# Latent attention of a three-layer transformer kernel: a new order of the score sets, the rotated parts and the PSUM copies on TensorE, VectorE and ScalarE

## What is computed

```python
def _mla(h, positions, w_in, q_a_norm_g, w_q_b, kv_a_norm_g, w_kv_b, w_out):
    ...
    q = (_rmsnorm(q_a, q_a_norm_g) @ w_q_b).reshape(b, s, MLA_HEADS, MLA_NOPE + MLA_ROPE)
    q_nope = q[..., :MLA_NOPE]
    q_pe = _rope(q[..., MLA_NOPE:], positions)
    k_pe = _rope(k_pe[:, :, None, :], positions)[:, :, 0]
    kv = (_rmsnorm(c_kv, kv_a_norm_g) @ w_kv_b).reshape(b, s, MLA_HEADS, MLA_NOPE + MLA_V)
    k_nope, v = kv[..., :MLA_NOPE], kv[..., MLA_NOPE:]
    scale = (MLA_NOPE + MLA_ROPE) ** -0.5
    def block(args):
        qn, qp = args
        sc = (jnp.einsum('bqhd,bkhd->bhqk', qn, k_nope, preferred_element_type=f32)
              + jnp.einsum('bqhr,bkr->bhqk', qp, k_pe, preferred_element_type=f32)) * scale
        p = jax.nn.softmax(sc, axis=-1)
        return jnp.einsum('bhqk,bkhd->bqhd', p.astype(v.dtype), v)
    o = _from_blocks(lax.map(block, (_to_blocks(q_nope), _to_blocks(q_pe))))
    o = o.reshape(b, s, MLA_WIDTH) * jax.nn.silu(z)
    return o @ w_out
```

## Time and profile before

| | |
|---|---|
| Median of 3 runs | 2895.57 us (2894.34 to 2899.68) |
| The profiled execution, own time | 2888.15 us |
| Its span in the trace | 2886.3 us |
| TensorE (PE) busy | 2741.3 us, 95% of the span |
| TensorE weight loads (PEld) busy | 2179.3 us, 76% |
| VectorE (DVE) busy | 1691.3 us, 59% |
| ScalarE (ACT) busy | 1320.9 us, 46% |
| Mean granted TensorE clock | 0.982 of full speed |

### The profile page before, as it was taken

One profiled execution on the slowest core, in us unless ns is written; L12 is line 12 of the kernel. 1 busy time (PEld: TensorE's weight loads), 2 busy tenths in 40 slices (PEclk: granted clock), 3 DMA queues, 4 the chain that ended last, 5 costly groups with the idle time before them and its releaser, 6 DMA issues.

```text
span 2886.3 us, 35234 instructions
## 1 busy us (share of the span) xinstructions
PE 2741.3 (95%) x13229; PEld 2179.3 (76%) x13229; DVE 1691.3 (59%) x2268; ACT 1320.9 (46%) x1902; POOL 0.2 (0%) x4
## 2 busy tenths in 40 slices
PE   7999999998899999999999889999999999999998
PEld 4777777776677777877877667666778888888887
DVE  7688888888777544444455635555765434334345
ACT  5676676665323244444443435565534223123233
POOL 0000000000000000000000000000000000000000
PEclk8999999999999999999999999999999999999999
DMA  7311111111445400000021310000311111111112
GB/s 250 110 46 46 35 51 44 51 36 58 152 155 168 141 10 12 14 6 9 7 102 53 111 44 29 24 16 15 103 38 50 45 53 46 50 47 42 53 41 87
DMA packets 218309, 176.78 MB, mean 61 GB/s; under 512 B 9610, under 2 KB 203106, under 8 KB 218210
## 3 DMA queue, kind: packets, MB, share of 16 engines
q1 hardware_dynamic: 216688, 171.07, 18.9%
q10 hardware_dynamic: 1522, 4.37, 0.4%
HBM read 158.12 MB, written 17.30 MB: 61 GB/s over the span
## 4 chain that ended last, share of the span: by engine, by line
PE 78%; DVE 8%; ACT 6%; DVEq 3%; DMA 2%; issue 2%; SPq 0%; ACTq 0%
PE PS L510 18%; PE PS L512 18%; PE PS L511 18%; PE PS L2195 4%; PE PS L1349 4%; PE PS L1336 2%; PE PS L1322 2%; DVE rest L502 1%; PE PS L1326 1%; PE PS L2185 1%; PE PS L2689 1%; PE PS L2702 1%; PE PS L2156 1%; DMA gated<-in_w_ada 1%; PE PS L2713 1%
## 5 line engine op out<-in xcount | busy, mean ns | idle before, releaser
L510 PE MATMUL PS<-h_high,w_high 128*128 128x512 f32 x2096 | 838.2, 400 | 25.3 <-DVE w_low L532 12.8
L512 PE MATMUL PS<-h_high,w_low 128*128 128x512 f32 x2096 | 822.4, 392 | 0.0
L511 PE MATMUL PS<-h_low,w_high 128*128 128x512 f32 x2096 | 822.1, 392 | 0.0
L510 PEld LDWEIGHTS PS<-h_high,w_high 128*128 128x128 f32 x2096 | 397.2, 189 | 115.1 <-issue 16.1
L512 PEld LDWEIGHTS PS<-h_high,w_low 128*128 128x128 f32 x2096 | 396.7, 189 | 85.0
L511 PEld LDWEIGHTS PS<-h_low,w_high 128*128 128x128 f32 x2096 | 397.6, 190 | 80.4 <-issue 1.4
L527 ACT ACTIVATE w_high<-raw_weights 128x1024 fp32r<-128x1024 f32 (+2 forms) x156 | 156.3, 1003 | 371.7 <-PE PS L512 369.3
L532 DVE TENSOR_TENSOR w_low<-raw_weights,w_high 128x1024 fp32r<-128x1024 f32 (+2 forms) x156 | 179.7, 1153 | 98.7 <-ACT w_high L527 98.4
L3336 DVE SCALAR_TENSOR_TENSOR gated<-rest,gated 128x1024 f32<-128x1024 f32 x44 | 56.6, 1286 | 238.1 <-ACT gated L3294 238.1
L1471 ACT ACTIVATE residual<-PS,rest 128x1024 f32<-128x1024 f32 x112 | 123.7, 1111 | 134.7 <-DVE rest L1633 134.6
L871 DVE SCALAR_TENSOR_TENSOR residual<-PS,rest,residual 128x512 f32 (+1 forms) x96 | 70.9, 749 | 171.1 <-PE PS L512 167.5
(11 more groups left out here) (376 smaller groups left out, 4141.3 us busy)
## 6 DMA issues: line engine op xcount, KB each, us to landing
raw_weights<-in_w_in SPq DMA_DIRECT2D x59, 512.0 KB, 4.1
raw_weights<-in_w_up SPq DMA_DIRECT2D x44, 512.0 KB, 3.8
gated<-in_w_ada SPq DMA_DIRECT2D x13, 1536.0 KB, 7.5
raw_weights<-in_w_out SPq DMA_DIRECT2D x24, 512.0 KB, 4.0
residual<-x_kept SPq DMA_DIRECT2D x3, 4096.0 KB, 14.2
rest<-in_ada_w SPq DMA_DIRECT2D x16, 576.0 KB, 4.9
activations<-in_ada_w SPq DMA_DIRECT2D x8, 1024.0 KB, 14.0
x_kept<-residual SPq DMA_DIRECT2D x2, 4096.0 KB, 14.5
```

Of the source, the lines that this page charges most:

```text
L510: e.matmul(out_, wh[:, k, :], xh[:, k, cols], start=first, stop=False)
L511: e.matmul(out_, wh[:, k, :], xl[:, k, cols], start=False, stop=False)
L512: return e.matmul(out_, wl[:, k, :], xh[:, k, cols], start=False, stop=last_k)
```

## The change

Four things are put in another order in the three functions; no instruction is added or taken out, except register moves of the sequencers that go with the order.

1. TensorE: in blocks 4 and 6 the sets Q1 and K1 stand ahead of PV(1) and PV(2) and no longer behind them. In block 2, PV(0) stays ahead of R1.
2. ScalarE: in block 7 of every head but the last, and in block 1 of even heads, the copy of the transposes stands ahead of the next exponential. In block 1 of odd heads the copy stands ahead of the ScalarE part of R0 (behind the exponential, as before).
3. VectorE, odd heads: the VectorE part of R0 goes from block 1 to block 2, behind the maximum there. That of R1 goes from block 2 to block 3, behind the division and ahead of the maximum. `dve_rope` goes from block 3 to 5, and `act_rope` from 3 to 4.
4. VectorE, even heads: `dve_rope` goes from block 1 to 2.

```diff
@@ pe_head
-                if q in (2, 4, 6):
-                    pe_pv(e, t, q // 2 - 1)
+                if q == 2:
+                    pe_pv(e, t, 0)
                 if wanted(t, BEFORE.get(q), more):
                     pe_set(e, t, BEFORE[q])
+                if q in (4, 6):
+                    pe_pv(e, t, q // 2 - 1)
@@ act_head
             for q in range(8):
+                copied = more and (q == 7 or (q == 1 and not t.odd))
+                if copied:
+                    act_evac(e, t, q)
                 if q < 7:
                     act_exp(e, t, q + 1)
...
-                if wanted(t, BEFORE.get(q), more):
+                if q != 1 and wanted(t, BEFORE.get(q), more):
                     act_set(e, t, BEFORE[q])
-                act_evac(e, t, q)
+                if not copied:
+                    act_evac(e, t, q)
+                if q == 1 and wanted(t, BEFORE[q], more):
+                    act_set(e, t, BEFORE[q])
                 if q == 1 and more and not t.odd:
                     act_rope(e, t, 1, t.lows)
-                if q == 3 and more and t.odd:
+                if q == 4 and more and t.odd:
                     act_rope(e, t, 0, t.lows + 2)
@@ dve_head
                 dve_probs(e, t, q)
+                if q == 3 and wanted(t, BEFORE[2], more):
+                    dve_set(e, t, BEFORE[2])
                 if q < 7:
                     dve_max(e, t, q + 1)
...
-                if wanted(t, BEFORE.get(q), more):
+                if q == 2 and wanted(t, BEFORE[1], more):
+                    dve_set(e, t, BEFORE[1])
+                if q == 2 and more and not t.odd:
+                    dve_rope(e, 1, 2 * t.half + 2)
+                if q == 5 and more and t.odd:
+                    dve_rope(e, 0, 2 * t.half + 3)
+                if q not in (1, 2) and wanted(t, BEFORE.get(q), more):
                     dve_set(e, t, BEFORE[q])
-                if q == 1 and more and not t.odd:
-                    dve_rope(e, 1, 2 * t.half + 2)
-                if q == 3 and more and t.odd:
-                    dve_rope(e, 0, 2 * t.half + 3)
```

## The result

The changed kernel takes 2872.22 us (median of 3 runs, 2870.30 to 2875.38) against 2895.57. The ratio of the runs is 0.9924, with a 95% interval of 0.9895 to 0.9953. The forecast was 2874.2. Six more runs of the changed kernel, beside 28 of the kernel before, gave a ratio of 0.9912 (0.9893 to 0.9932).

What follows compares the result with a forecast made beforehand. TensorE's list was taken to bound the stretch from 1049 to 1450 us. Gains of 12.5 + 7.3 + 5.9 = 25.7, less 5.9 for new waits, plus 1.5 for the clock, gave 21.3 us and 2874.2 us, range 2866 to 2883.

Steps and rivals of the forecast that it cites:

- Copies: Blocks 7 and 1: all 14 waits of PV for the copy of transposes go, 12.5 us won.
- The division: Block 3 of odd heads: T(3) no longer waits for the division behind R1's VectorE part, 7.3 us won.
- K1 ahead of PV(2): Head changes: seven waits of S(0) for K1's low part go, 5.9 us; K0's low part has 0.49 us to spare.
- the second rival: K1's product waits for K0's low part, so the 5.9 us stay lost; time 2880, chance 7%.
- What is late next: Odd heads, blocks 2 to 4: new waits of 1.6 us, 2.0 with restarts, per head; 5.9 us given back.
- All four late starts: Odd heads: waits of 0.5 us before R1's product, 0.5 before T(3), 0.3 before Q0's product, 0.3 before Q1's.
- The 0.1 us for each restart: Odd heads: each new wait costs 0.1 us beyond its length, as after the wait of PV.
- The clock: Odd heads: with no wait over 1 us left, the clock's fall in one loop turn goes, 1.5 us won.
- The sum: Whole kernel: 25.7 - 5.9 + 1.5 = 21.3 us won, nearly 1% of the kernel and 5% of the stretch.
- the first fell: Rival: odd heads win nothing, as their new chain of waits brings the loss back; 14.6 us won, 2881, chance 10%.
- Something did arrive: Rival denied here: nothing arrives, as what follows the stage waits for something else; time 2895.6, chance 4%.
- the clock did not drop over the stretch: Rival denied here: granted clock falls to 0.92 over the stretch, 401 us growing by some 32; time 2906, chance 3%.

Runs made afterwards that it cites:

- the copies alone: Kernel before with only ScalarE's new order of the copies, `act_rope` left in block 3; ratio 0.9994, stretch 444.8 us.
- the order that removes all four late starts: Changed kernel with stage ends and clears reordered, then odd heads: R1 behind T(2), Q0 ahead of PV(1), Q1 behind T(4); 2857.99 us, ratio 0.9858.
- the rotated parts alone: Kernel before with only VectorE's new order of the R0 and R1 parts and both rope moves; ratio 0.9961, stretch 443.9 us.
- the sets alone: Kernel before with only Q1 and K1 ahead of the values in blocks 4 and 6; ratio 0.9987, stretch 449.3 us.

## Why the prediction was right

*Copies.* The step of 12.5 us held: all 14 waits went, and putting the copies back costs 1.62 us an even head, or 0.78 at the turn and 0.84 in block 1, as summed. The step also said, of odd heads, that the copy frees PV(0). What it is worth there depends on the rest: with the copies alone, 1.11 of the 1.14 us by which PV(0) started earlier came back as a longer wait of T(3).

*The division.* Gone, at 7.3 us. Of the three parts its removal costs the most: the changed kernel loses 13.0 us of stretch without it, a fall of the clock in each odd head included, or some 12 by the estimate without falls, against 11.4 for the copies.

*K1 ahead of PV(2).* The seven waits went and no wait of K1's product came: the 0.49 us to spare held, and the second rival fell. Put back, it costs 0.86 us an even head, forecast 0.84; in odd heads it costs 0.62, as Q1's late start goes at the same time.

*What is late next.* All four late starts are there, in the order given, 1.5 us against 1.6. The 0.1 us for each restart, taken from PV, was too much: the order that removes all four late starts won 1.57 us an odd head (55.62 to 54.05), so the restarts added under 0.1 to the 1.5 and not 0.4. So 4.7 us were given back and not 5.9.

*The clock.* Right in kind, but the forecast says that the lower level shows in one place of the stretch, and the first profile has it in three, two of them in head 0. The 1.5 us is what the fall in head 3 of the first profile cost (61.01 against 59.46), and no loop turn of the changed kernel had one in two profiles.

*The sum.* By clean heads the change is worth 3 x 3.83 + 4 x 2.71 = 22.3 us, where the forecast had 25.7 - 5.9 = 19.8. The difference is 1.2 us of late starts and restarts, and 0.8 for the late T(3) of even heads: the forecast gave no term to the move of `dve_rope` there, and this late start of 0.2 us is drawn as no idle time and so stood in no row of the waits. The other 0.5 is spread over steps of some hundredths. With 1.5 for the clock it is 23.8, and the medians say 23.4. That these two agree to half a microsecond is in part luck: the other measured difference is 26.3, and the stretch shrank by 25.1, of which 1.6 is a fall of the clock that the first profile has ahead of head 0's T(0) (8.09 us from the first scores) and the second has not (6.53). The forecast counted no fall there.

*The rivals.* Odd heads kept 3.8 of their 5.3 us, so the first fell. It was the nearest: with the copies alone the gain of block 1 does come back at T(3), as it says, though the rotated parts alone won 1.62 us. Something did arrive, and the clock did not drop over the stretch. The Trainium skill, page "TensorE: Matmul & The Clock Gate", section "A second HAM failure mode: psum-queue depth-cycling", has short idle times between groups of matmuls make the clock swing; for the waits of this stretch the measurement says otherwise. In the stretch, in all twelve traces, no wait of 1.1 us or less is followed by a fall, and the first kernel alone has 21 of them there.

## What to carry to other kernels

When one engine's list is the bound, reorder for the engine that feeds it as a whole: walk the chain with measured durations from one of its starts to the next, and ask after each cure what is late then. A single move in such a schedule can be worth nothing or less, and its worth must be read from lengths of like pieces of the trace, since a kernel of 2.9 ms scatters by more than the move. Small late starts hide behind the drawn length of a matmul: take distances between starts, not idle figures.

## What the runs showed that I had not expected

The clock's falls differ from one execution to the next, but not at every wait. Behind the waits of 2.3 us before T(3) it fell in one of three heads of the first kernel and two of three with the sets alone; behind 3.4 us, in two of three and three of three; behind 0.2 to 1.1 us, never in this stretch. It fell to 1.2 GHz for a while each time (granted clock 0.83 over ten us) and cost a head 1.55 to 1.63 us where it hid no other wait.

A wait of 1.1 us is not safe everywhere. Each of the twelve traces has one of 1.09 to 1.13 us between 887 and 895 us, in an earlier part of the program, and in three of them the clock fell within 2 us behind it. This is the one in the run with the copies put back, with the granted clock (last figure but two):

```profile
893.17 0.83 PE L1145 MATMUL PS<-rest 128*128 128x1 f32 x6 [1.10 <-DVE rest L502]
890.00:900.00 10.00, 8.90 (x36) 6.95 (x35) 9.21 (x14) 1.59 (x2) 0.00 (x0) 0.83 1.03 419
```

Between 749 and 754 us nine traces have a wait of 1.6 to 1.7 us, and the clock fell behind all nine. What makes these places differ from the stretch no run here shows.

A fall can also pay for a wait: in five odd heads the slower TensorE hid the 1.2 us that Q1's product would otherwise have waited, and with the sets alone such a head was only 0.4 us longer than one without a fall. In head 0, V1 waits 2.02 us in the first trace, where the scores ahead of it ran at half clock for a time, and 2.64 in most others. A fall ahead of it is not enough for that, though: in two traces in which the clock fell right at the first scores, V1 waited 2.64 and 2.65 us.

The kernel before, unchanged, took between 2886.5 and 2902.0 us in 28 runs. It was traced once, so how its head lengths repeat over these runs is not shown; in the two traces of the changed kernel they agree to 0.03 us for heads 1 to 6.
